# One layer's modulation is moved into the layer before it, in a hybrid mLSTM / latent / differential attention trunk

## What is computed

```python
def _layer(x, cond, lp, lam_init, ctx):
    mod = jax.nn.silu(cond) @ lp["w_mod"] + lp["b_mod"]        # (1024 -> 6144), from cond alone, not from x
    sh1, sc1, g1, sh2, sc2, g2 = jnp.split(mod[:, None, :], 6, axis=-1)
    h = _rms(x, lp["norm1_g"]) * (1.0 + sc1) + sh1
    z = h @ lp["w_in"]
    ...   # three mixers (mLSTM, latent attention, differential attention), gated and merged into y
    x = x + g1 * (y @ lp["w_out"])
    h2 = _rms(x, lp["norm2_g"]) * (1.0 + sc2) + sh2
    return x + g2 * (jnp.square(jax.nn.relu(h2 @ lp["w_ff1"])) @ lp["w_ff2"])
```

## Time and profile before

| | |
|---|---|
| time, 3 runs | 2922.69 us median (2919.51 to 2923.07) |
| the profiled execution | span 2919.1 us, about that of the fastest run (2919.51) and 3.6 us under the median |
| PE busy | 2739.9 us, 94% of the span |
| PEld, DVE, ACT, POOL busy | 84%, 45%, 24%, 44% |
| DMA | 215.13 MB, mean 74 GB/s |
| mean granted PE clock | 0.972 of full speed |

### The profile page before, as it was taken

The page is one execution under the profiler, slowest core; times in us unless marked ns, Lnnn a source line. Parts: engine busy times, 40 slices in busy tenths (PEclk is TensorE's granted clock), DMA queues, the critical chain, the costliest instruction groups (busy, mean ns, idle before and its releaser), DMA issues.

```text
span 2919.1 us, 46013 instructions
## 1 busy us (share of the span) xinstructions
PE 2739.9 (94%) x17468; PEld 2439.4 (84%) x17468; DVE 1317.6 (45%) x1748; ACT 696.5 (24%) x1190; POOL 1289.1 (44%) x580
## 2 busy tenths in 40 slices
PE   5999998998999899999989999999899998999996
PEld 3954897786999799999958469968779998999996
DVE  4324326697223644253233342467772256353352
ACT  2122333505321211011022223253153112010011
POOL 1501452150565466666534025513405654666663
PEclk8999999999999999999979999999999999999998
DMA  6222121020122322222242411201102223222221
GB/s 252 80 92 79 53 75 37 16 71 17 59 73 69 109 76 72 72 79 72 76 164 71 138 40 60 74 16 37 65 9 73 73 70 109 75 72 73 78 72 50
DMA packets 61647, 215.13 MB, mean 74 GB/s; under 512 B 6832, under 2 KB 10160, under 8 KB 61232
## 3 DMA queue, kind: packets, MB, share of 16 engines
q1 hardware_dynamic: 56448, 203.97, 20.8%
q10 hardware_dynamic: 5040, 8.99, 0.9%
HBM read 208.44 MB, written 4.49 MB: 73 GB/s over the span
## 4 chain that ended last, share of the span: by engine, by line
PE 78%; DVE 10%; ACT 3%; DVEq 3%; issue 3%; DMA 2%; ACTq 1%; POOL 0%; POOLq 0%; SPq 0%
PE big L399 19%; PE big L403 19%; PE big L402 19%; PE big L532 4%; PE last_two L563 2%; PE two L546 2%; DVE sq L1491 2%; PE big L635 1%; PE last_two L659 1%; DMA raw<-in_w 1%; PE big L422 1%; PE big L660 1%; PE big L425 1%; PE big L426 1%; PE two L480 1%
## 5 line engine op out<-in xcount | busy, mean ns | idle before, releaser
L358 POOL TENSOR_TENSOR w_hi<-raw,cst 128x1024 fp32r<-128x1024 f32 x288 | 555.4, 1928 | 1549.5 <-PE big L399 1189.1
L399 PE MATMUL big<-act_hi,w_hi 128*128 128x320 f32 x2784 | 878.5, 316 | 27.2 <-DVE act_lo L1560 9.6
L402 PE MATMUL big<-act_lo,w_hi 128*128 128x320 f32 x2784 | 869.4, 312 | 0.0
L403 PE MATMUL big<-act_hi,w_lo 128*128 128x320 f32 x2784 | 869.2, 312 | 0.0
L361 POOL TENSOR_TENSOR w_lo<-raw,w_hi 128x1024 fp32r<-128x1024 f32 x288 | 733.6, 2547 | 44.1 <-issue 8.0
L399 PEld LDWEIGHTS big<-act_hi,w_hi 128*128 128x128 f32 x2784 | 530.4, 191 | 35.7 <-issue 16.7
L402 PEld LDWEIGHTS big<-act_lo,w_hi 128*128 128x128 f32 x2784 | 530.8, 191 | 1.5 <-issue 0.4
L403 PEld LDWEIGHTS big<-act_hi,w_lo 128*128 128x128 f32 x2784 | 530.0, 190 | 0.0
L399 PE MATMUL big<-ff_hi,w_hi 128*128 128x320 f32 x1024 | 316.9, 309 | 4.1 <-DVE ff_lo L1150 4.1
L402 PE MATMUL big<-ff_lo,w_hi 128*128 128x320 f32 x1024 | 315.3, 308 | 0.0
L403 PE MATMUL big<-ff_hi,w_lo 128*128 128x320 f32 x1024 | 315.2, 308 | 0.0
(11 more groups left out here) (293 smaller groups left out, 3676.3 us busy)
## 6 DMA issues: line engine op xcount, KB each, us to landing
raw<-in_w SPq DMA_DIRECT2D x384, 512.0 KB, 3.3
x<-in_x ACTq DMA_DIRECT2D x1, 2560.0 KB, 10.8
out_y<-x SPq DMA_DIRECT2D x8, 320.0 KB, 2.4
cst<-in_const ACTq DMA_DIRECT2D x1, 1938.5 KB, 16.3
small<-in_small ACTq DMA_DIRECT2D x2, 505.0 KB, 4.5
out_C<-c_new ACTq DMA_DIRECT2D x2, 256.0 KB
v_d<-in_past ACTq DMA_DIRECT2D x2, 256.0 KB, 2.8
k_d<-in_past ACTq DMA_DIRECT2D x2, 256.0 KB, 3.0
```

What stands on the lines that cost most here:

```text
L358: nc.gpsimd.tensor_tensor(w_hi[:, to, :], raw[:, slot, :], ones[:, 0:1].to_broadcast([P, BLK]), ALU.mult)
L399: first = mm(ps, wh, ah, start=k == 0, stop=False)
L402: mm(ps, wh, al, start=False, stop=False)
L403: last = mm(ps, wl, ah, start=False, stop=k == nk - 1)
```

## The change

Five things, all in one edit:

1. All loops are unrolled: waits have constants in place of registers, `Fori` and its branches are gone. The same order of weights is now given by `ring_order()`.
2. Layer 1's 48 mod blocks stand in the ring between the first 48 dense blocks of layer 0's feed-forward stage, one behind each. PE does `mod_block` after each of those projections, and a fold in every fourth; ACT has a `keep_row` for each chunk between its relus. `mod` becomes `mods`, with room for both layers. In layer 1 nothing of the modulation is left: not at its start, not in the mLSTM loop, not at norm 2.
3. The next norm's scale and squares follow each tile in the last feed-forward chunk, as norm 2 had them; the last norm of the program has its squares there too. Norm 1 now uses the form of norm 2 (`scale_x`, then `shift_and_split`): eight tiles are scaled before, not after, the multiplication by `rs`.
4. Layer 0's first 16 mod blocks have a place of their own (`first_mod`, 64 KB a partition, over buffers used later) and are loaded without a wait, ahead of the ring.
5. ACT's first DMAs: a small early part of the constants, then x, `small`, and the rest of the constants.

```diff
+def ring_order():
...
+        if l:
+            out += dense(l, 1, FF_A + 1)
+        else:
+            out += dense(0, 0, SPLIT) + mod(0, MOD_A, MOD_A + 4) + dense(0, SPLIT, DENSE_A)
+            out += mod(0, MOD_A + 4, MOD_BLOCKS - 8) + dense(0, DENSE_A, FF_A + 1) + mod(0, MOD_BLOCKS - 8, MOD_BLOCKS)
+        following = dense(l, FF_A + 1, DENSE) + (dense(l + 1, 0, 1) if l + 1 < DEPTH else [])
+        for n, block in enumerate(following):
+            out += [block] + (mod(l + 1, n, n + 1) if l + 1 < DEPTH and n < MOD_BLOCKS else [])
...
@@ SP
+            for n in range(MOD_A):
+                sp.dma_start(first_mod[:, n, :], first_d[n]).then_inc(first_mod_loaded[n // 4], 16)
+            for place, block in enumerate(ORDER):
+                if place >= RAW:
+                    kind, of, index = ORDER[place - RAW]
+                    if kind == "mod":
+                        sp.wait_ge(mod_block_used, of * MOD_BLOCKS + index + 1)
+                    else:
+                        sp.wait_ge(split_ready, of * DENSE + index + 1)
...
@@ PE
+            def mod_block(l, n, out):
+                c, q = divmod(n, 4)
+                if l == 0 and n < MOD_A:
+                    pe.wait_ge(first_mod_loaded[c], 64)
+                    src = first_mod[:, n, :]
...
-            with pe.Fori(0, DEPTH) as l:
...
+            for l in range(DEPTH):
+                if l == 0:
...
+                    mod_rows(0, 4, two[:, 1, 0:256])
+                else:
+                    sums(l, FIRST_USE["norm1"], FIRST_SQ["norm1"], KD, 1)
+                    pe.wait_ge(mod_kept, 3)
...
-                    if i % 5 == 3 and u < 5:
+                    if l == 0 and i % 5 == 3 and u < 5:
...
+                for c in range(FF_CHUNKS):
+                    use, block = FIRST_USE["ff"] + 16 * c, FIRST_BLOCK["ff"] + 16 * c
+                    for m in range(16):
...
+                        n = 16 * c + m
+                        if l + 1 < DEPTH and n < MOD_BLOCKS:
...
+                            mod_block(l + 1, n, two[:, n // 4 % 2, 0:256])
+                        if l + 1 < DEPTH and n % 4 == 1 and 4 < n < MOD_BLOCKS + 4:
+                            mod_fold(l + 1, n // 4 - 1, one[0][:, 2 * n - 10:2 * n - 2])
...
@@ ACT
+                for c in range(FF_CHUNKS):
+                    relu(c, 0)
                     for m in range(8):
                         if m + 1 < 8:
-                            relu(m + 1)
-                        round_ff(m)
-            act.wait_ge(layer_open, DEPTH + 1)
-            squares(DEPTH, 0, [x[:, k, :] for k in range(KD)], None)
+                            relu(c, m + 1)
+                        round_ff(c, m)
+                        if m == 0:
+                            next_row(4 * c - 1)
+                        if m == 4:
+                            next_row(4 * c)
+                    next_row(4 * c + 1)
+                    next_row(4 * c + 2)
...
+                squares(l + 1, FIRST_SQ["norm1"], x_tiles, lambda k: l * SOURCES + 16 + k + 1)
@@ DVE
+                    for m in range(KD):
+                        scale_x(scale1, m)
+                shift_and_split(l, "norm1", "h1", 0)
...
                     for m in range(8):
-                        add_to_x(l, FIRST_USE["ff"] + 8 + m, m, 5, c * 8)
-                dve.drain().then_inc(layer_open, 1)
+                        add_to_x(l, FIRST_USE["ff"] + 16 * c + 8 + m, m, 5)
+                        if last_c:
+                            dve.drain().then_inc(src_ready, 1)
+                            if l + 1 < DEPTH:
+                                scale_x(scale1, m)
+                            gather(l + 1, FIRST_SQ["norm1"], m - 1)
```

More of the change, by code:

```diff
@@ L54, with mod, dense @@
     DENSE += _n
-BLOCKS = MOD_BLOCKS + DENSE
 RAW, SPLIT = 4, 2
[L57 to L71, removed]
+assert DENSE % SPLIT == 0
+MOD_A, DENSE_A, FF_A = 16, FIRST_BLOCK["acq"], FIRST_BLOCK["ff"]
+def ring_order():
+    def mod(l, a, z):
+        return [("mod", l, n) for n in range(a, z)]
+    def dense(l, a, z):
+        return [("dense", l, n) for n in range(a, z)]
+    out = []
+    for l in range(DEPTH):
[7 more added lines that the diff above has]
+            out += [block] + (mod(l + 1, n, n + 1) if l + 1 < DEPTH and n < MOD_BLOCKS else [])
+    return out
+ORDER = ring_order()
+PLACE = {block: place for place, block in enumerate(ORDER)}
+assert len(PLACE) == DEPTH * (DENSE + MOD_BLOCKS) - MOD_A
 USE_STAGES = [("norm1", 1), ("mv", 2), ("mg", 1), ("mq", 2), ("mk", 2), ("mo", 4),
@@ L316, in _ @@
         def _(sp):
[L317 to L341, removed]
+            for n in range(MOD_A):
[7 more added lines that the diff above has]
+                        sp.wait_ge(split_ready, of * DENSE + index + 1)
+                sp.dma_start(raw[:, place % RAW, :], w_d[place]).then_inc(raw_loaded[place % RAW], 16)
             for k in range(KD):
@@ L1121, in _ @@
[L1121 to L1133 removed]
+                if l == 0:
+                    keep_row(0, MOD_CHUNKS - 1, two[:, 1, 0:256])
@@ L1282, in _ @@
                 for k in range(KD + 1):
                     if k < KD:
+                        v.tensor_tensor(y[:, k, :], y[:, k, :], rs[:, :], ALU.mult).then_inc(whole, 1)
+                    if k:
+                        dve.wait_ge(hi_done, l * SPLITS + FIRST_SPLIT[split_name] + k)
                         for g, a, b in GROUPS:
[L1285 to L1286 removed]
@@ L1644, in _blocks @@
         out += [f1[8 * c:8 * c + 8], _pairs(_tiles(f2[D * c:D * c + D]))]
-    kinds = {"mod": _wide(i["w_mod"][l]),
-             "dense": np.concatenate([np.stack(o) if isinstance(o, list) else o for o in out])}
-    return np.stack([kinds[kind][index] for kind, index in ORDER])
+    dense = np.concatenate([np.stack(o) if isinstance(o, list) else o for o in out])
+    return {"mod": _wide(i["w_mod"][l]), "dense": dense}
 def _columns_of(a):
@@ L1736 @@
     tokens = np.concatenate([i["x_prompt"][0], i["x_sample"][0]])
+    blocks = [_blocks(i, l) for l in range(DEPTH)]
     arrays = {
@@ L1743 @@
         "in_past": np.stack([_past(i, l) for l in range(DEPTH)]),
-        "in_w": np.stack([_blocks(i, l) for l in range(DEPTH)]),
+        "in_first": blocks[0]["mod"][:MOD_A],
+        "in_w": np.stack([blocks[l][kind][index] for kind, l, index in ORDER]),
     }
```

374 lines of the change are left out of this document (200 added, 174 removed).

## The result

The change makes the kernel slower: 2929.66 us (median of 10 runs, 2927.28 to 2932.1) against 2920.51 (10 runs, 2916.62 to 2924.66), a ratio of 1.0029 (95% interval 1.0021 to 1.0037). The forecast was 2917, faster by 0.2%, with a range from 2898 to 2935: the time lies in the range, the direction is wrong.

What follows compares the result with a forecast made beforehand. PE was taken to bound the kernel: its stream plus the places where it waits. Terms of 53.5 - 27.5 - 13.5 - 0.1 - 8 - 7 - 3 gave -5.6 from 2922.7, so 2917.1 us, range 2898 to 2935.

Steps and rivals of the forecast that it cites:

- term 1: Layer 0's feed-forward stage: added mod blocks, folds and waits for ACT's copies, less mid-chunk waits; +53.5 us (+42 to +66).
- the mid-chunk waits: Layer 0's feed-forward stage: PE's 0.5 us waits go in three places where a mod block stands over them; -2.1 us.
- rival B: PE pays more at each border of a mod block, 1.1 us per block: 2934 us, slower; chance 0.19.
- Term 6: Unrolling, mostly four register operations on the chain of each mLSTM unit: -7 us (-12 to 0).
- Term 4: Norm 2: layer 1 loses chunk and folds but bares the table load, -0.4; layer 0 +0.3; together -0.1 us.
- term 5: End of program: squares following the tiles shorten PE's wait and make the last sums 1.2 to 1.5 shorter; -8 us.
- border: Between layers: 20 mod blocks and the back edge gone, 16.1 us in place of 43.6; -27.5 us.
- the 1.2 for POOL beside DVE: At the border of layers: 1.2 us added for POOL's split running beside DVE's multiplication.
- mLSTM loop: Layer 1's mLSTM loop: five mod chunks and their folds leave the chain of units; -13.5 us (-15 to -9).
- end: Last norm of the program: its squares follow the tiles, so PE waits less for the last sums; -8 us.
- start: First projection begins earlier than 60.58, since layer 0's first 16 mod blocks get their own place; -3 us.
- Rival D: Gains outside hidden: start bound by DVE's scalings, unrolling gives nothing, mLSTM chunk partly in a wait; 2928 us, chance 0.19.

Runs made afterwards that it cites:

- copies_early: Changed kernel with two of ACT's copies of a finished mod chunk moved ahead in the feed-forward stage: 2915.89 us, ratio 0.998.
- unroll_only: Kernel before the change with its loops unrolled and nothing else: 2917.92 us, ratio 0.9989.
- folds_late: Changed kernel with early copies, mod blocks in fours, early Ln table load, and folds of chunks 4 to 11 moved to the border: 2891.08 us, ratio 0.9899.
- no_layer1_mod: Changed kernel without any of layer 1's modulation (blocks, loads, copies, folds); layer 1 uses layer 0's modulation vector: 2870.43 us, ratio 0.9822.
- copies_table: copies_early plus a tiny one-column Ln ahead of the wait for the sums in the large norms: 2911.31 us, ratio 0.9961.
- Fours_busy: Changed kernel with early copies, mod blocks in fours, early Ln table load, and unread matmuls ahead of three sums: 2898.28 us, ratio 0.9924.

## Why the prediction was wrong, step by step

The sum came to -5.6; the two profiled executions differ by +9.5, the medians by +9.2. The parts were nearly all named; the 15 us between stand in three terms. No one of them turns the direction clear of noise by itself: term 1 at its measured size gives +0.5, with the unrolling at -2.5 it is +5.0.

1. **Term 1, feed-forward stage: the step that failed is the sum of its parts, which had no half clock behind the waits.** 53.5 forecast, 59.6 measured. A mod block was 0.76 for 0.74 (+0.9), a fold 0.91 for 0.9, the six waits 9.3 for 9.2. Missing were three stretches at half clock behind them, 4.6 together, and the mid-chunk waits gave back 1.5 in place of 2.1: the block that holds one takes 0.90 more than its neighbours before, 0.41 more after, at three places. (36.5 + 10.8 + 9.3 + 4.6 - 1.5 = 59.7.) The prediction allowed for PE paying more only in rival B, inside the mod blocks; it was paid behind ACT's late copy. Both costs went with one edit in copies_early. Rival B, dearer blocks, did not happen (0.76, far from the 0.98 that it needed): the slower result has another mechanism than the rival for it.

2. **Term 6, unrolling: mis-sized, -2.5 for -7.** The step that failed is "on the chain of a unit of the mLSTM loop four register operations stand", each counted as a gain. The chain lists them, but three lie beside an activation of the same engine that is still running, and unroll_only shows 0.09 a unit for 0.36. On the profiles' side this term is 8.3 off: with the chunks' 13.5 taken out, the mLSTM loops and the mixers came out 1.3 longer, not 7 shorter. The changed kernel's layer 0 had gained 1.5 in its mLSTM loop and was 4.0 longer in the stretch of the mixers and first projections. That this goes with the clock, the traces of the unrolled kernels show, which all run the same mixers in layer 0: by the granted clock PE is at half speed for 17 us of layer 0's mixers in copies_early, unroll_only and folds_late, and their stretch takes 787.9 to 788.3; in the changed kernel and the nine others it is 20 to 24 us, and the stretch takes 791.5 to 795.3.

3. **Term 4, norm 2: in layer 1 +2.0 for -0.4.** The bared table load was forecast, and costs 1.25 to 1.34 at each of four places (copies_table). What was left out is that the removed chunk kept PE busy ahead of the sums, which reached over 1.96 before and 3.87 now. With sums at full clock (no_layer1_mod) the norm is 0.3 shorter than before, as forecast. Fours_busy, with work put back there, has them at full clock; but two of the eight traces without any have it too, so the half clock is likely where the chunk is missing, and not certain. The prediction had the same fact in term 5 (cold sums cost 1.2 to 1.5 more) and did not ask it of the place that loses its chunk.

The rest held: border 28.6 for 27.5 (the 1.2 for POOL beside DVE was not there: two multiplications in 1.74), mLSTM loop 13.5 between unroll_only and the changed kernel for 13.5, end 8.3 for 8, start 2.6 for 3. The border's 15.04 is in part luck of the clock: in copies_early, whose edit does not touch the border, the sums took 3.36 in place of 1.96 and the border 16.45, against the 16.1 of the sum. The Trainium skill's rule on the shared pair of ports ("SBUF — State Buffer", Terms) had nothing to act on at this border: POOL has its two slots filled by then and does not split from 1511.4 to 1529.2. The Trainium skill's rule on taken branches ("Runtime: NRT & Kernel Launch", Instruction fetch mechanics) would by itself, by the prediction's estimate, have made unrolling worth 7 us more. No run shows that: unrolling is worth 2.5 us in all, and the feed-forward stage, with three of the edges in it, takes 463.79 with them and 463.69 without.

Rival D, with its 2928, names a time 1.7 us from the measured one, but by luck: of its three causes only the small gain from unrolling came true; the start and the mLSTM loop gained what the sum has.

Three readings in the prediction are wrong and did not decide. A block of 48 matmuls takes 7.04 from start to start, not 7.1 to 7.2; the stage's mean is higher because the first block, which still waits for norm 2's tiles, takes 16.8. The border announces three additions and sums two. The parts of term 1 by their own bounds reach from 28 to 71, not from 42 to 66, and no reason for the narrower range is given.

What stays open: with every term at its measured size, and -2.5 for the unrolling, the sum is about +5.7; the 3.5 us to the +9.2 of the medians lie, as far as the traces show, in the half clock in the mixers, and why the changed kernel should have more of it in the median is not shown. Nor is it shown why three of six waits were followed by half clock: a wait close ahead, or a longer one, goes with it, but six cases prove nothing. How the start's 2.6 us divide between the place for 16 blocks and ACT's earlier loads was not tested.

## What to carry to other kernels

Work that is put into a stage bound by PE is paid in full, so place it by its changes of kind: a group of four small blocks cost 0.52 each, a single one 0.76, and what can wait until PE idles anyway costs nothing: eight folds moved to the border made the stage 7.1 shorter and the border no longer. A producer on another engine should deliver between two blocks, not behind its next heavy pair; ask of each wait that an order makes whether the clock falls behind it. Before a register or queue piece of the chain is counted as a gain, look whether the engine's previous instruction is still running beside it.

## What the runs showed of the hardware

- Eight full matmuls of 320 columns in fp32 reach over 1.96 us from first to last start at full clock and 3.87 at half. At norm 2 of layer 1 they were at half clock, all or in part, behind an idle stretch of 3.13 us in six of eight traces, and in none of six in which PE had work up to 1.2 us before. In the changed kernel a wait of 1.35 to 1.92 us between blocks was followed by about 3.6 us at 0.53 of the clock in three of six cases.
- With constant waits the wait for the sums stands on the table load ahead of the activation (978.42 in unroll_only, behind the sums), where with a wait on a register it stood on the activation (table load at 979.40 in the kernel before, ahead of the sums). Where nothing else hides it this costs the 1.28 us of the load, 1.25 to 1.34 measured; an activation on one column ahead of the wait (0.20 us) takes it off the path.
- Executions of one unrolled kernel spread over 12 us (2912.6 to 2925.2 in unroll_only), more than most single steps here are worth; layer 1's feed-forward stage takes 463.68 to 463.79 in all 14 traces.
